# Sparse attention in a three-block transformer kernel: the next head pair's compressed steps placed singly among the present pair's wide steps, with two PSUM banks for values and six for steps

## The reference, cut to what matters

```
lc  = q @ kc.T + bias(distance to the block's end)     # 31 compressed keys
o_c = masked_softmax(lc) @ vc
ls  = q @ k_selected.T + bias;   o_s = masked_softmax(ls) @ v_selected
lw  = q @ k_window.T + bias;     o_w = masked_softmax(lw) @ v_window
out = gate0 * o_c + gate1 * o_s + gate2 * o_w
```

## Time and profile before

| | us |
|---|---|
| median of 3 runs | 2111.53 (2109.34 to 2111.93) |
| the profiled execution, its own time | 2109.28 |
| its span | 2107.9 |
| PE busy in the span | 2053.5 (97%) |
| DVE, ACT, POOL busy | 1047.4, 808.2, 257.3 |
| the stretch 1498 to 1640 of the span, PE busy in it | 142.0, 134.06 |
| DVE, ACT, POOL busy in that stretch | 90.56, 85.67, 84.73 |

### The profile page before, as it was taken

How to read it: one execution, slowest core, us unless ns; L and a number is a source line. 1 busy time by engine, 2 the same in 40 slices (tenths; PEclk the granted TensorE clock), 3 DMA queues, 4 the chain that set the end, 5 groups by cost and what they waited for, 6 DMA issues and landing times.

```text
span 2107.9 us, 25685 instructions
## 1 busy us (share of the span) xinstructions
PE 2053.5 (97%) x10399; PEld 1665.8 (79%) x10399; DVE 1047.4 (50%) x1890; ACT 808.2 (38%) x1533; POOL 257.3 (12%) x330
## 2 busy tenths in 40 slices
PE   7999999999999999999999999999999999999998
PEld 7867788888888767788888888888766788888887
DVE  6474454324437475454334446746566445433443
ACT  5255452222224355452222235344456333322322
POOL 3124410000001114210000000000366000000000
PEclk9999999999999999999999999999999999999999
DMA  5433333333223322233333232422321324323331
GB/s 167 113 72 78 98 100 99 97 95 100 91 95 95 95 62 71 70 106 96 94 100 99 87 95 63 110 60 80 86 61 33 93 80 126 99 90 102 98 95 65
DMA packets 271674, 190.69 MB, mean 90 GB/s; under 512 B 19740, under 2 KB 241108, under 8 KB 271556
## 3 DMA queue, kind: packets, MB, share of 16 engines
q1 hardware_dynamic: 264080, 174.28, 28.3%
q0 software_dynamic: 7328, 14.72, 3.0%
q10 hardware_dynamic: 148, 0.04, 0.0%
HBM read 183.72 MB, written 4.24 MB: 89 GB/s over the span
## 4 chain that ended last, share of the span: by engine, by line
PE 86%; DVE 7%; ACT 4%; issue 1%; POOL 1%; DMA 1%; DVEq 0%; ACTq 0%; POOLq 0%
PE bank L635 50%; PE bank L681 8%; PE bank L683 8%; PE bank L682 8%; PE bank L781 3%; PE bank L748 2%; PE bank L767 2%; DVE weights_hi_lo L1041 1%; DVE arena L1475 1%; ACT weights_hi_lo L1753 1%; DVE x_residual L1195 1%; PE bank L866 1%; ACT arena L1812 1%; PE bank L868 1%; PE bank L867 1%
## 5 line engine op out<-in xcount | busy, mean ns | idle before, releaser
L635 PE MATMUL bank<-h_features,weights_hi_lo 128*128 128x512 f32 (+1 forms) x5112 | 1114.4, 378 | 8.2 <-DVE weights_hi_lo L1041 6.8
L635 PEld LDWEIGHTS bank<-h_features,weights_hi_lo 128*128 128x128 f32 x5112 | 917.6, 189 | 189.2 <-DVE weights_hi_lo L1041 8.9
L1041 DVE TENSOR_TENSOR weights_hi_lo<-weights,weights_hi_lo 128x1024 fp32r<-128x1024 f32 (+2 forms) x337 | 395.6, 1179 | 489.8 <-ACT weights_hi_lo L1753 489.3
L1753 ACT ACTIVATE weights_hi_lo<-weights 128x1024 fp32r<-128x1024 f32 (+2 forms) x337 | 337.7, 1007 | 273.4 <-PE bank L683 247.9
L681 PE MATMUL bank<-weights_hi_lo,hidden 128*128 128x512 f32 x528 | 205.9, 390 | 0.0
L683 PE MATMUL bank<-weights_hi_lo,hidden 128*128 128x512 f32 x528 | 205.4, 389 | 0.0
L682 PE MATMUL bank<-weights_hi_lo,hidden 128*128 128x512 f32 x528 | 205.4, 389 | 0.0
L1869 ACT ACTIVATE arena<-arena 128x512 f32<-128x512 f32 x66 | 41.7, 632 | 270.2 <-DVE arena L1205 270.2
L2245 POOL TENSOR_SCALAR arena<-arena,row_stats 128x256 f32<-128x256 f32 (+5 forms) x140 | 127.3, 921 | 139.7 <-DVE row_stats L1125 63.7
L1205 DVE TENSOR_TENSOR arena<-bank,arena 128x512 f32<-128x512 f32 x66 | 69.5, 1054 | 118.8 <-PE bank L635 109.1
L1872 ACT ACTIVATE hidden<-arena 128x512 fp32r<-128x512 f32 x66 | 41.7, 632 | 217.9 <-DVE arena L1211 217.9
(11 more groups left out here) (363 smaller groups left out, 2071.6 us busy)
## 6 DMA issues: line engine op xcount, KB each, us to landing
weights<-in_w_in_dram SPq DMA_DIRECT2D x78, 512.0 KB, 4.0
weights<-in_w_gate_dram SPq DMA_DIRECT2D x66, 512.0 KB, 3.8
weights<-in_w_up_dram SPq DMA_DIRECT2D x66, 512.0 KB, 3.8
weights<-in_w_down_dram SPq DMA_DIRECT2D x60, 512.0 KB, 3.6
weights<-in_w_out_dram SPq DMA_DIRECT2D x24, 512.0 KB, 3.7
bias_rows<-decay_scratch POOLq DMA_DIRECT2D x16, 256.0 KB, 4.3
weights<-in_w_in_dram SPq DMA_DIRECT2D x13, 256.0 KB, 3.3
weights<-in_w_down_dram SPq DMA_DIRECT2D x12, 256.0 KB, 2.6
```

The lines of the kernel that those rows point to most:

```text
L635: last = e.matmul(out_ap, l, r, start=(j == 0), stop=(j == len(pairs) - 1))
L1041: e.tensor_tensor(pair_view(i, 1), raw_view(i), pair_view(i, 0).bitcast(F32), ALU.subtract).then_inc(done, tick(("split", i)))
L1753: e.activation(pair_view(i, 0), raw_view(i), ACT.Copy).then_inc(done, tick(("hi", i)))
```

## The change

The list of steps is built in another order. The compressed steps of pair 0 still come first (0 to 3). Those of pair rr+1 are then placed inside pair rr: after t2 and after t3 of the selected branch, and after t2 and t3 of the window branch. So a block of twelve reads t0 t1 t2 C0 t3 C1 t0 t1 t2 C2 t3 C3, at steps 4 to 15, 16 to 27 and 28 to 39; steps 40 to 47 are the eight wide steps of pair 3, as before. Since the first value product of the next pair (its compressed group) now comes one slot behind the last one of the present pair, the values get two banks (6 and 7, used in turn) and the steps six (0 to 5). The bias loads of POOL now start after the last step that reads the pair's rows, which is t3 of the window branch at step 14 or 26.

```diff
+            def compressed(rr, t):
...
+                if t == NT - 1:
+                    read[2] = ("M", rr, "cmp")
+                    groups[len(steps) - 1] = Group(read[2], kept[-NT:], ...
+            kept = []
+            for t in range(NT):
+                compressed(0, t)
             for rr in range(NR):
...
-                for t in range(NT):
-                    nw = ((t + 1) * P - CMP_BLOCK) // CMP_STRIDE + 1
...
+                        if t >= 2 and rr < NR - 1:
+                            compressed(rr + 1, 2 * (br - 1) + t - 2)
...
-            banks = Ring(PSUM, known(4), {None: list(range(8)), "step": list(range(7)), "values": [7]})
+            banks = Ring(PSUM, known(4), {None: list(range(8)), "step": list(range(7)), "values": [7], "sparse step": list(range(6)), "sparse values": [6, 7]})
...
-                        out_ap = bank(g.bank, "values")
+                        out_ap = bank(g.bank, "values" if cycle[0] == "step" else "sparse values")
...
-                    cycle[0] = "step"
+                    cycle[0] = "sparse step" if s == "M" else "step"
...
+                    last_of = {u.bias_use: i for i, u in enumerate(steps)}
...
-                            if u.bias is not None and (i == n or steps[i].bias_use != u.bias_use) and u.bias_use + 4 < first + 8:
+                            if u.bias is not None and last_of[u.bias_use] == i - 1 and u.bias_use + 4 < first + 8:
```

More of the change, by code:

```diff
@@ L531, in nsa_steps @@
                                           NGT[:, t, 3 * rr + br:3 * rr + br + 13:12]))
[L532 to L541, removed]
+                        if t % 2 == 1:
+                            products = []
+                            for kt in range(t + 1):
+                                c0 = P if kt == t else 0
+                                for j, r in enumerate(halves):
+                                    at = base + HD * j
+                                    products.append((r, 256 * hf + c0, 256 * hf + 256, VSW[:, kt, at:at + HD], NSA_P[hf][:, j, kt, c0:256], False, br == 2 and kt == NT - 1))
+                            read[hf] = ("M", rr, br, hf)
+                            groups[len(steps) - 1] = Group(read[hf], [u for u in steps if u.name[0:3] == ("M", br, rr) and u.t // 2 == hf], products, name, T,
+                                                           False, br == 2 and hf == 1, rr, hf)
+                        if t >= 2 and rr < NR - 1:
+                            compressed(rr + 1, 2 * (br - 1) + t - 2)
             return steps, groups
@@ L617, in bank @@
                 def bank(name, group=None, held=0.6):
-                    use = banks.take(name, group or cycle[0], turn[0] + held if cycle[0] == "step" and group is None else None)
+                    use = banks.take(name, group or cycle[0], turn[0] + held if cycle[0] is not None and group is None else None)
                     pe.wait_ge(*banks.vacant(use))
```

9 lines of the change are left out of this document (added).

## The result

The changed kernel takes 2115.63 us (median of 11 runs, 2114.33 to 2119.6), the kernel before 2111.41 us in the same comparison (11 runs). The medians differ by 4.2 us. The ratio of the times on record, which is not the quotient of these two medians, is 1.0026, with a 95% interval from 1.0017 to 1.0035: 5.5 us, from 3.6 to 7.4. So the changed kernel is slower, by some 4 to 6 us, where 5.5 had been forecast. 2115.63 lies in the range given (2111.5 to 2120.5).

The account below looks back on a forecast made before the run. PE, busy for 97% of 2107.9 us, was taken as the bound. Waits of 9.8 us come and 4.2 go, +5.6, taken as +5.5; on the median of 2111.53 us that gave 2117.0 us, range 2111.5 to 2120.5.

Parts of the forecast that it names:

- (a): Slot 7: the fill cannot start sooner, so PE reaches it with less done and loses 0.7 us.
- (b): Slots 9, 21, 33: value products wait for ACT's copy behind a 512-key step's exponentials; 1.16 us three times, 3.5 us.
- (c): Slots 11 and 35, behind a gate: the fill waits for the bank of t2's second head; 0.8 us twice, 1.6 us.
- (d): Slot 18: value products wait for ACT's copy behind t0's exponentials, the gate and 256-key exponentials; 1.5 us.
- (e): Slot 26 (scores need a bank the gate empties) and slot 30 (DVE's copy behind a fill's product); 0.8 us together.
- (f): Slots 39 to 41, no fill at 39: PE waits while POOL scales t2, C2 and t3 in a row; 1.7 us.
- waits that go: Idle PE time between 1525 and 1610 us, half of it POOL waits at slots 14, 26, 38; 4.2 us credited.
- (g): Bias loads for pairs 2 and 3, issued later and needed at slots 19 and 31; they cost zero.
- (h): Value banks: with two of them PE waits zero; with one it would wait for two operations behind every pair.
- rival with a chance of 0.10: Banks: t2's turns at slots 9, 21, 33 wait, six places up to 0.5 us each; +8.5, 2120.0 us.
- rival on the other side: Faster or unchanged: ACT stays ahead, (b) to (e) vanish, the bubbles go; -1.8 us, 2109.7 us; chance 0.15.
- half of it: Rival: (b), (a) and (f) come, the gate's backlog hides (c), (d), (e); +1.7, 2113.2 us; chance 0.15.

Follow-up runs that it names:

- e3: Changed kernel's step order with the old banks (seven for steps, one for values); 2117.53 us, ratio 1.0037 to the kernel before.
- e1: Kernel before, step order kept, with only the new bank division (six for steps, two for values); 2112.69 us, ratio 1.0010 to the kernel before.
- e7: Changed kernel with ScalarE's three gate rows divided, the last two one slot later; 2111.98 us, ratio 1.0009 to the kernel before.
- e4: Changed kernel with the fourth gate fill moved from slot 31 to slot 39; 2113.71 us, ratio 1.0017 to the kernel before.
- e5: Changed kernel with ScalarE's copy ahead of the slot's exponentials in all slots without a fill, except 49; 2113.26 us, ratio 1.0009 to the kernel before.
- e6: Changed kernel with ScalarE's copies first and the fourth gate fill at slot 39; 2111.30 us, ratio 1.0001 to the kernel before.
- e8: Changed kernel with ScalarE's gate rows divided and its copies first; 2111.20 us, ratio 1.0003 to the kernel before.
- e9: Changed kernel with copies first, gate rows divided and the fourth gate fill at slot 39; 2108.99 us, ratio 0.9991 to the kernel before.
- e10: Kernel before, old order and banks, with copies first, gate rows divided and fourth gate fill at slot 39; 2114.73 us, ratio 1.0020 to the kernel before.

## Why the prediction came out right, step by step

The mechanism is that of the forecast: GpSimd's bubbles go, and in the new order ScalarE's copy stands behind work that is longer than what PE has to do meanwhile. The terms against the waits that the first profile of after shows (the second has the same within 0.01 us each):

| term | forecast | measured |
|---|---|---|
| (a) slot 7 | 0.7 | 0 there |
| not forecast: scores of slot 6 | 0 | 0.48 |
| (b) slots 9, 21, 33 | 3.5 | 2.6 (3 x 0.87) |
| (c) slots 11, 35 | 1.6 | 1.4 |
| (d) slot 18 | 1.5 | 1.68 |
| (e) slots 26, 30 | 0.8 | 1.0 (0.23, 0.78) |
| (f) slots 39 to 41 | 1.7 | 1.5 (0.16, 0.70, and 0.66 that VectorE ended) |
| waits that go | 4.2 | 4.4 |
| sum | +5.6 | +4.3 |

(b) The count from the start of the scores (3.32 to the copy, 0.62 more to the products) was exact: 1521.79 + 3.94 = 1525.73, the instant in the row above. PE came 0.3 later than counted, since the turn ahead took 1.10 us; in e3, with the seventh bank, it took 0.88 and the wait 1.10. So 0.2 us of each of the three waits lies inside the turn, by reason of the banks, which I had priced at nothing. The products start at the instant that the queue allows in either case, and with these 0.2 us the term is 3.3, close to the forecast of 3.5.

(a) is the term that failed. I held that the fill of slot 7 could not start sooner than its bank allows, so that the scores taken out ahead of it would be lost time. From the first turn of slot 4 the fill begins after 4.31 us in after and after 4.96 in e1, which has the same banks, nearly the same clock there (0.94 and 0.96) and the 512-key scores ahead of the fill. So the fill moved forward by the work that was taken out, and PE did not wait ahead of it. The wait of 0.48 us at slot 6 is no stand-in for the term, for e1 has it too.

(g) held: the list has no wait of PE at slots 19, 20, 31 and 32, where late bias loads would have shown.

(h) was half right. The value banks cost nothing and are worth a lot (e3), but six step banks are no longer enough everywhere: 0.48 us at slot 6 (e1: 0.47, and none in before's second profile), 0.23 at slot 26, and (c). In the old order they cost 1.6 us, which the prediction gave to a rival with a chance of 0.10. That rival had the place wrong (turns at slots 9, 21 and 33) but not the idea.

(d) and (f) are shown by taking their cause away (e7, e4). For (b) and (c) it is shown that ScalarE's queue is the nearest limit: the value products of slots 9, 21 and 33 wait for it in none of e5, e6, e8 and e9, and the fills of slots 11 and 35 not in e7. It is not the only one. Limits that stand close behind, a bank or VectorE's copy, take back more than half of what these two terms cost (the table of e9), and the forecast had no word on them. Of (e), the 0.78 of slot 30 was put down to the wrong engine.

The rival on the other side (2109.7) is refuted by the waits: ScalarE is busy for 78.80 of 137.90 us, and PE waits for it by 6.7 us (2.61 + 1.68 + 0.78 + 1.4 + 0.23). Of "half of it" (2113.2) the gate's part did not hide: (c) came with 1.4 us and (d) with 1.68. That the sum came out only 1.3 us from the forecast is in part luck: (a), 0.7 us, did not come, and the 0.48 us of slot 6, which stands in no term, did. No further fall of the clock came in the stretch. The Trainium skill (Perfetto Trace Analysis, Optimization Strategy) says that a repeated equal gap on the engine that should be saturated can mean a lack of SBUF or PSUM. The runs agree for one pair of gaps: the two of 0.71 us at the fills of slots 11 and 35 went with a seventh step bank (e3), though almost no time was won. For the others they do not: the three of 0.71 that GpSimd ended stayed at six banks (e1), and the three of 0.87 stayed at seven (e3, 1.10 each). The loss that the prediction drew from this rule for six banks did come, 1.6 us in the old order (e1), as unequal waits of 0.2 to 0.9 us.

## What to carry to other kernels

When steps are reordered for one engine, count for every other in-order engine what now stands between its input and the one result that the first engine waits for; its mean load says nothing (at slot 20 ScalarE had been idle for 4 us just ahead of the exponentials that made its copy late). A short operation that someone waits for belongs ahead of long ones that nobody waits for yet, and long work that only has to free a bank can be divided, its freeing part first. Such edits are to be tried together and in the order that they are meant for: here they were worth 1.0 to 2.3 us singly, 6 together, and a loss in the old order. And when one engine's late result is mended, look at what is ready just behind it: the next limit can give most of the time back.

## What was not expected of the hardware

The clock falls at other places in other executions of one program. The sparse attention begins, in code that is the same up to there in all kernels of the study, between 1497.62 us (e3) and 1503.68 us (first profile of after) from the start; from its last value products to the end every profile looked at has 469.7 or 469.8 us. The 10.4 us between the first two spans are so 5.7 ahead of the stretch, 4.65 in it and nothing behind it. In the 20 us from 740, for instance, the granted clock is 0.91 in the first profile of after and 1.00 in the second.

At one place all profiles show a fall, behind the thin matmuls ahead of slot 0: the fill of slot 3 takes 5.49 us at a granted clock of 0.50 (the lower level, 1.2 of 2.4 GHz) in most and 4.3 in three, one of them. Elsewhere in the attention a fall came twice, and both times behind 5 to 7 us in which PE stood still for a quarter of the time. That alone does not bring one, as will be seen. In e10 it is in the windows above; in e3:

```profile
1616.00:1621.00 5.00, 3.68 (x23) 2.05 (x21) 2.42 (x10) 1.43 (x6) 2.73 (x2) 1.00 0.19 56
1621.20:1625.30 4.10, 4.10 (x21) 2.36 (x20) 2.66 (x9) 2.10 (x8) 4.08 (x4) 0.60 0.00 0
```

It costs: value products that take 0.87 us at the full clock took 1.54 there. But in the first profile of after PE is busy for 3.32 of the 5.00 us from 1548.80, with the wait of slot 18 in them, and in e3 itself for 6.26 of the 9.00 us from 1541.00: it stands still for longer, the granted clock is 1.00, and no fall follows. The Trainium skill (TensorE: Matmul & The Clock Gate, What's actually happening) calls the lower clock the default that activity lifts; these two places agree with that, and the two without a fall show that idle time in itself does not tell where one comes. What sets it off was not measured.
